# Sparse attention's half of the odd layer's output projection, unit by unit inside the attention loop

## The reference, cut to what matters

```
def odd_layer(h, ...):
    proj = rms_norm(h, norm_mix) @ w_in
    y_c = rwkv7_time_mix(proj_c, ...)              # 8 heads x 64, a state over time
    y_d = dsa_attention(q, k, v, qi, ki, wi)       # 8 query heads x 64, top-64 keys
    h = h + jnp.concatenate([y_c, y_d], axis=-1) @ w_out
    return h + moe_swiglu(rms_norm(h, norm_ffn), router, e_gate, e_up, e_down)
```

## Time and profile before

| | us |
|---|---|
| median of 3 runs | 1525.81 |
| lowest, highest | 1525.42, 1528.82 |
| span of the profiled execution | 1527.9 |
| PE busy | 1448.0 |
| DVE busy | 653.7 |
| ACT busy | 259.0 |
| POOL busy | 30.3 |

### The profile page before, as it was taken

The page is one execution under the profiler, slowest core; times in us unless marked ns, Lnnn a source line. Parts: engine busy times, 40 slices in busy tenths (PEclk is TensorE's granted clock), DMA queues, the critical chain, the costliest instruction groups (busy, mean ns, idle before and its releaser), DMA issues.

```text
span 1527.9 us, 46201 instructions
## 1 busy us (share of the span) xinstructions
PE 1448.0 (95%) x21517; PEld 1382.4 (90%) x21517; DVE 653.7 (43%) x1549; ACT 259.0 (17%) x441; POOL 30.3 (2%) x33
## 2 busy tenths in 40 slices
PE   7998999997986889999999999999999999999997
PEld 6857999997864778999999999999999999999996
DVE  6952554445467651343224224134224323332327
ACT  2333444434234210200000000000000000000001
POOL 0000000000000210000000000000000000000000
PEclk9998999999996999999999999999999999999998
DMA  9041655353330008699999999999999999999994
GB/s 312 30 166 56 220 206 181 128 198 124 126 109 1 3 3 321 236 392 406 408 395 406 409 388 408 408 381 408 408 380 410 408 376 409 406 386 408 408 373 169
DMA packets 138184, 434.27 MB, mean 284 GB/s; under 512 B 10108, under 2 KB 13286, under 8 KB 137863
## 3 DMA queue, kind: packets, MB, share of 16 engines
q1 hardware_dynamic: 133536, 420.59, 71.5%
q0 software_dynamic: 1472, 5.24, 1.0%
q10 hardware_dynamic: 2982, 5.45, 1.0%
HBM read 426.42 MB, written 4.85 MB: 282 GB/s over the span
## 4 chain that ended last, share of the span: by engine, by line
PE 85%; DMA 6%; DVE 6%; ACT 3%; issue 1%; SPq 0%; ACTq 0%; DVEq 0%
PE bank L2545 34%; PE bank L2543 18%; PE bank L2152 4%; PE bank L2154 4%; PE bank L2153 4%; DMA ring<-in_moe_w_up 4%; PE bank L1894 3%; PE bank L2222 3%; DMA ring<-in_moe_w_gate 2%; PE bank L2125 2%; PE bank L2140 1%; PE bank L2060 1%; PE bank L2145 1%; PE bank L2387 1%; DVE xnT L1083 1%
## 5 line engine op out<-in xcount | busy, mean ns | idle before, releaser
L2543 PE MATMUL bank<-ring,yT 128*32 128x384 f32 x5760 | 633.5, 490 | 7.0 <-DMA ring<-in_moe_w_gate 4.3
L2545 PE MATMUL bank<-ring,yT 128*32 128x128 f32 x5760 | 634.9, 273 | 0.0
L2545 PEld LDWEIGHTS bank<-ring,yT 128*32 128x32 f32 x5760 | 627.7, 110 | 0.4 <-issue 0.4
L2545 PE MATMUL bank<-ring,arena 128*32 128x128 f32 x2304 | 255.4, 273 | 0.0
L2543 PE MATMUL bank<-ring,arena 128*32 128x384 f32 x2304 | 255.2, 490 | 0.0
L2545 PEld LDWEIGHTS bank<-ring,arena 128*32 128x32 f32 x2304 | 251.4, 110 | 0.0
L1801 DVE TENSOR_TENSOR arena<-arena,bank 128x384 f32<-128x384 f32 x56 | 28.9, 551 | 430.6 <-PE bank L2545 286.7
L1749 DVE STREAM_TRANSPOSE arena<-arena 32x192 f32<-32x192 f32 x384 | 141.9, 370 | 114.3 <-PE bank L2545 109.3
L2543 PEld LDWEIGHTS bank<-ring,yT 128*32 128x32 f32 x5760 | 165.9, 108 | 9.7 <-issue 5.9
L2154 PE MATMUL bank<-arena_r,ring_r 128*128 128x256 f32 x608 | 171.5, 282 | 0.0
L2152 PE MATMUL bank<-arena_r,ring_r 128*128 128x256 f32 x528 | 148.0, 280 | 1.3 <-DVE arena_r L1329 1.3
(11 more groups left out here) (473 smaller groups left out, 1264.0 us busy)
## 6 DMA issues: line engine op xcount, KB each, us to landing
ring<-in_moe_w_gate SPq DMA_DIRECT2D x56, 2048.0 KB, 22.0
ring<-in_moe_w_up SPq DMA_DIRECT2D x56, 2048.0 KB, 22.1
ring<-in_moe_w_down SPq DMA_DIRECT2D x56, 2048.0 KB, 20.3
ring<-in_ffn_w_gate SPq DMA_DIRECT2D x5, 2048.0 KB, 7.9
ring<-in_ffn_w_up SPq DMA_DIRECT2D x5, 2048.0 KB, 8.1
ring<-in_ffn_w_down SPq DMA_DIRECT2D x5, 2048.0 KB, 8.6
ring<-in_o_w_in SPq DMA_DIRECT2D x5, 2048.0 KB, 7.7
ring<-in_e_w_in SPq DMA_DIRECT2D x4, 2048.0 KB, 16.9
```

The lines of the kernel that those rows point to most:

```text
L2543: pe_.matmul(b[QUAD[m], 0:FM], x(m), w[:, 0:FM], start=start, stop=stop, skip_group_check=True)
L2545: last = pe_.matmul(b[QUAD[3], P * m:P * m + P], x(m), w[:, FM:FB], start=start and m == 0, stop=stop, skip_group_check=True)
```

## The change

Inside each turn of the attention loop, between the products with the values and the transposes, PE now multiplies the unit that is finished (u-3) with its 128 rows of `w_out`, for all 8 output tiles: 8 products of 128 x 128 into banks 0 and 1 (first 128 tokens) or 2 and 3 (last). The last unit's comes after the loop, in the place of the three warming products. ACT copies the two banks into `sparse_out` (in buffers named raw and relu) once for each half of the tokens, and DVE adds them to `hT` behind L1558. The final output projection is left with the RWKV half, 4 products for each output tile. The sums of squares and half of the transposed norms move to bank 4. POOL's key mask waits for the triangles of both halves of the heads.

```diff
+    sparse_out = [L1[n][:, 0:KD * P] for n in ("raw", "relu")]
+    KK_BANKS = (4, 0)
...
             pool.wait_ge(sem("mk_raw"), t + 1)
+            pool.wait_ge(sem("T_ready"), 2 * t + 2)
             mk = sc["L"].rearrange("p (h x) -> p h x", h=HEADS)
...
+        def sparse_copy(t):
+
+            act.wait_ge(*step(f"sparse{t}_done"))
+            act.wait_ge(*((sem("acc_done"), NT) if t else (sem("shifted"), 7)))
+            for b in range(2):
+                last = act_.activation(sparse_out[t][:, 512 * b:512 * b + 512], bank[2 * t + b][:, :], ACT.Copy)
+            last.then_inc(step(f"sparse{t}_copied")[0], 1)
+
         for u in range(2, UNITS + 2):
             odd_attention(u)
+            if u == UNITS - 1:
+                sparse_copy(0)
             rwkv_step(u - RWKV_LAG)
         for u in range(UNITS + 2 - RWKV_LAG, UNITS + 2):
             rwkv_step(u)
+        sparse_copy(1)
...
-                link(v.tensor_tensor(kk2, kk2, bank[u - 6][:, :], MUL))
+                link(v.tensor_tensor(kk2, kk2, bank[KK_BANKS[u - 6]][:, :], MUL))
...
                 sem("WT_copied"), 1)
+            dve.wait_ge(*step(f"sparse{t}_copied"))
+            h_t = hT[:, :, t * P:t * P + P]
+            link(v.tensor_tensor(h_t, h_t, sparse_out[t].rearrange("p (k n) -> p k n", k=KD), ADD))
             dve.wait_ge(sem("lora_loaded"), 16 * 5)
...
                 last.then_inc(sem("pv_done"), 1)
+            if between:
+                between()
             if 1 <= u <= UNITS:
...
         def out_projection(n, behind):
             for i in range(KD):
-                if i % 4 == 0:
-                    loaded(n + i // 4)
-                for k in range(KD):
+                for k in range(KM):
...
+        def project_sparse(w):
+
+            if w < 0:
+                return
+            f, t = unit(w, UNITS)
+            if w == 0:
+                pe.wait_ge(sem("gates_done"), 1)
+                loaded(NOUT)
+                loaded(NOUT + 1)
+            pe.wait_ge(sem("o_copied"), UNITS + w + 1)
+            for i in range(KD):
+                last = pe_.matmul(bank[2 * t + i // 4][:, (i % 4) * P:(i % 4) * P + P],
+                                  view(NOUT + i // 4)[:, KM + f, (i % 4) * P:(i % 4) * P + P],
+                                  yT[:, KM + f, t * P:t * P + P], start=(f == 0 and i % 4 == 0), stop=(f == KM - 1),
+                                  skip_group_check=True)
+            if f == KM - 1:
+                last.then_inc(step(f"sparse{t}_done")[0], 1)
...
-                      lambda kt, h: Vd[:, kt, :], L1["pT"], dsa_first)
+                      lambda kt, h: Vd[:, kt, :], L1["pT"], dsa_first, between=lambda: project_sparse(u - 3))
...
                 pe.wait_ge(*step("kk_wide"))
                 for k in range(KM):
+                    if k == 2:
+                        pe.wait_ge(*step("sparse0_copied"))
                     for t in range(NT):
                         i = t * KM + k
-                        last = pe_.transpose(half(bank[k // 2], k)[:, t * P:t * P + P],
+                        last = pe_.transpose(half(bank[KK_BANKS[k // 2]], k)[:, t * P:t * P + P],
                                              sc["tmp"][:, i * P:i * P + P], ident)
                 last.then_inc(step("kk_back")[0], 1)
-        keep_warm(bank[6], WARM["tilde"])
+        project_sparse(UNITS - 1)
         pe.wait_ge(*step("tilde_done"))
+        pe.wait_ge(*step("sparse0_copied"))
...
             for hh in range(2):
+                if hh and not t:
+                    pe.wait_ge(*step("sparse1_copied"))
```

More of the change, by code:

```diff
@@ L167, in trunk @@
              "rwkv_prep": ["kk_raw", "L_done", "rk_done", "kk_inv", "tilde_done"],
-             "rwkv_act": ["kk_sq", "exps_done", "kk_norm", "kk_wide"],
+             "rwkv_act": ["kk_sq", "exps_done", "kk_norm", "kk_wide", "sparse0_copied", "sparse1_copied"],
              "routing": ["sel_ready", "m12_done", "work_ready"],
-             "rwkv_turned": ["kk_ss", "kk_back"]}
+             "rwkv_turned": ["kk_ss", "sparse0_done", "kk_back", "sparse1_done"]}
     def step(name):
@@ L910, in rwkv_step @@
                 act.wait_ge(*step("kk_ss"))
-                act_.activation(L1["st8"][:, 0:16], bank[0][:, 0:16], ACT.Sqrt).then_inc(step("kk_norm")[0], 1)
+                act_.activation(L1["st8"][:, 0:16], bank[4][:, 0:16], ACT.Sqrt).then_inc(step("kk_norm")[0], 1)
             elif u == 4:
@@ L2017, in _, with attention @@
         S5_STEPS = {"C": turn_c, "X": chunk_u, "G": turn_g, "S": chunk_states, "K": step_kernels, "out": turn_outputs}
-        def attention(u, base, q, k, vals, pT, first, p=None):
+        def attention(u, base, q, k, vals, pT, first, p=None, between=None):
             if u < UNITS:
@@ L2121, in out_projection @@
             for i in range(KD):
-                if i % 4 == 0:
-                    loaded(n + i // 4)
-                for k in range(KD):
+                for k in range(KM):
                     last = pe_.matmul(half(bank[2 + i // 2], i), view(n + i // 4)[:, k, (i % 4) * P:(i % 4) * P + P],
-                                      yT[:, k, :], start=(k == 0), stop=(k == KD - 1))
+                                      yT[:, k, :], start=(k == 0), stop=(k == KM - 1))
                 if i % 2:
@@ L2302, in _ @@
                     t, k = i // KM, i % KM
-                    last = pe_.matmul(bank[0][:, 2 * i:2 * i + 2], tmp4[:, k, t * P:t * P + P], C("pair"),
+                    last = pe_.matmul(bank[4][:, 2 * i:2 * i + 2], tmp4[:, k, t * P:t * P + P], C("pair"),
                                       start=True, stop=True)
```

## The result

| | us |
|---|---|
| before, median of 4 runs (lowest, highest) | 1527.24 (1525.42, 1528.82) |
| after, median of 4 runs (lowest, highest) | 1517.12 (1512.92, 1518.98) |
| ratio after / before, 95% interval | 0.9928 [0.9905, 0.995] |
| span of the profiled execution, before and after | 1527.9, 1514.5 |

The change is 10.1 us faster by the medians and 13.4 by the two profiled spans. The forecast was 12.4 faster, at 1513.4; the range, 1508 to 1520, holds the result. The profiled execution of the changed kernel took 1516.33, 1.8 more than its span, and in every other run where both are known the time is 1.8 to 1.9 above the span. So the profiled execution of before took about 1529.7 (an estimate from its span). That is 3.9 above the 1525.81 from which the forecast was made and outside the range of those three runs, not 2.1 above and inside it.

The account below looks back on a forecast made before the run. The prediction took PE's own order to bound the path ahead of the experts, and the weight stream, by a little, the experts. Projection -14.3, loop +4.9 and mask -3.0 gave -12.4 from 1525.8: 1513.4 us, 80% range 1508 to 1520.

Parts of the forecast that it names:

- Half of the projection: Final output projection: 64 of 128 records go at 0.2234 us each, all on the path, 14.3 us faster.
- The stream lets the gain through: Experts' weights: the stream moves with the experts' start; blocks 1 to 6 need 30.5 us and 41 are left.
- The loop: Attention loop: the sparse products added there delay RWKV's start by 4.9 us, one above the full-clock replay; bounds +2.5 and +15.2.
- full-clock replay: End of the attention loop: PE's order replayed at 2.4 GHz from turn 7, RWKV starting at 498.0 instead of 494.15, +3.85 us.
- The mask: Triangles on DVE: with POOL's mask waiting, L1539 is no longer stretched; 1.0 us gained in the first half, 2.0 in the second.
- full-clock rival: Loop and rounds: loop costs only 3.85 us, no clock fall after the triangles saves 1.5 more; 1510.8 us, chance 0.13.
- The addition, the renaming: DVE's two additions to `hT` (1.22 us each) fit into its idle time, and renaming the banks moves nothing: 0 us.
- The lower clock all the way: Attention loop: the clock stays low through all the last units, loop +15.2 us, 1523.7 in all; chance 0.05.
- the slower outcome: Loop and first half's rounds: low clock reaches into five rounds, 22.4 us lost against 17.3 saved; 1530.9, chance 0.03.
- the stream: Experts: their weight stream cannot move with its start, most of 12 us returns as PE waits; 1522 or more, chance 0.03.
- midway rival: Attention loop: the clock is up again only near 490, RWKV starts some 8 us late; 1516.5 us, chance 0.14.
- the mask's collision: POOL's mask in its new place stalls the first L1547 in each half, +4.7 us; 1518.1 us, chance 0.04.

Follow-up runs that it names:

- e8: Changed kernel with the final projection over all eight input tiles again, sparse half added twice, so another output: 1533.94 us, ratio 1.0031 to before.
- e4: Changed kernel with ACT's first copy of the sparse banks one turn earlier, in turn 6: 1515.56 us, ratio 0.9911 to before.
- e5: On top of e4, the last two units' sparse products moved behind the loop, ahead of the final projection, replacing eight warming products: 1511.93 us, ratio 0.9881 to before.
- e1: Changed kernel run again without an edit: 1519.21 us, ratio 0.9933 to before.
- e3: Changed kernel without the line that makes POOL's key mask wait for the triangles: 1521.48 us, ratio 0.9943 to before.
- e10: Changed kernel traced again without an edit, second of three such looks: 1513.79 us, beside 1528.58 for before.
- e2: Kernel before with only POOL's key mask waiting for the triangles: 1527.38 us, ratio 0.9983 to before.
- e6: Changed kernel with eight more warming products in PE's waits in turns 4 to 6 of the attention loop: 1517.33 us, ratio 0.9919 to before.
- e9: Changed kernel traced again without an edit, first of three such looks: 1517.9 us, beside 1528.58 for before.
- e11: Changed kernel traced again without an edit, third of three such looks: 1516.88 us, beside 1528.58 for before.

## Why the prediction was right, and where its sizes were off

*Half of the projection, -14.3.* Measured -13.81 between the marks. The mechanism is as forecast. A record was priced at 0.2234, from a row's 7.15, which runs to the last end; to the next row's start the same 32 records took 6.99 (590.59 to 597.58), 0.218 each, so 64 are 14.0. The slow start was 0.1 longer after. e8 isolates the term.

*The stream lets the gain through.* Right for the changed kernel. From the first expert product on it took 903.5 to 906.2 us in eleven traces of the kernels with the right output, with starts between 603 and 621 and no order by the start; before had 904.57 (and e8 908.47). PE's waits for weights come to 6.1 after and 5.6 before, all behind 1000 us.

*The loop, +4.9.* Measured +4.08 in the first trace, +4.1, +4.1, +4.8 and +5.9 in the others of this kernel: the mean is 4.6. The full-clock replay gave 3.85 and followed PE row by row: it put RWKV's start 2.7 behind `tilde_done`, the trace has 3.0, and the wait for ACT's copy, priced at 1.2 with PE as the later one, is 1.23. e4 and e5 confirm both by taking them away (1.47 and 2.03). The extra for units at the lower clock was the right kind: the clock was at 0.50 in the loop's first turns, rose behind unit 0, fell behind the sums of squares in turn 4 and rose again behind or inside unit 2. In e1, e3 and e10 it fell once more, at 480.7 to 481.5, and caught unit 3, which costs up to 1.8. The forecast had looked for the lower clock at units 3 and 4; it was at 0 and 2 in every trace, and at 3 in some.

*The mask, -3.0.* Right in size: -1.12 and -1.93 in e2, and by its ratio 2.6 with an interval of 0.8 to 4.4. In the first half I had taken 1.0 as net of ACT's second copy; net it is 0.54, since the copy costs 0.58. In the second half 2.0 was forecast for 1.93. But the second half gained 3.47 in the changed kernel, 1.54 more than the mask, and that is the clock in the rounds. Busy times and granted clock (the PEclk column) in the rounds of the second half, before, in the first trace of the changed kernel, and in e2:

```profile
540.00:543.00 3.00, 3.00 (x62) 3.00 (x62) 1.10 (x3) 0.00 (x0) 0.00 (x0) 0.50 0.00 0
536.00:545.00 9.00, 7.63 (x180) 6.59 (x180) 6.96 (x20) 3.05 (x6) 2.35 (x1) 1.00 0.01 2
538.00:540.00 2.00, 2.00 (x44) 2.00 (x42) 0.75 (x2) 0.00 (x0) 1.10 (x1) 0.50 0.00 0
```

The sum put this at nothing and left it to the full-clock rival, at 1.5. That size is right, but its reason, triangles in time, is not enough: e2 and e6 have the mask's wait too, the clock fell in their rounds, and they took 42.78 and 42.77 against 41.24. Of the ten traces with both the wait and the sparse half, e6 is the only one with that fall. What decides it stays open.

In the four cases in which the mask ran beside L1539 (before, and L1553 in e3), the stretched instruction ended 0.27 to 0.29 behind the mask, though it had started anything from 0.2 to 1.3 behind the mask's start. This agrees with the lock that the Trainium skill describes ("SBUF — State Buffer", "SBUF: two separate sides"): of a VectorE instruction with two SBUF inputs and a GpSimd one, the first holds the shared ports for its whole length and the other waits. With the wait in place the instructions with two SBUF inputs are no longer stretched, and L1562, with one, takes 0.42 to 0.45 beside a 2.35 mask. Whether the addition to `hT` would collide by the same rule was not put to the test: the two were 0.15 us apart.

*The addition, the renaming.* 0, as forecast; DVE idles 0.60 behind the addition.

*The sum.* By the marks the parts ahead of the experts sum to -13.7, against -12.4 forecast; the clock in the rounds is the term that the sum lacked. By the medians the gain is 10.1 (first runs) and 9.9 (e1), and the time is 3.7 above the forecast: 1.4 because the base of 1525.8 was too low (1527.24 with a fourth run; 33 later runs have medians of 1529.1 and 1528.8), and 2.3 because the gain was smaller. That it still lies 2.9 inside the range owes something to the range's width of 12. The two profiled spans differ by 13.4. All 38 runs of before have a median of 1528.8, and the 12 of the changed kernel 1517.8: 11.0 apart. The profiled execution of before lies 0.9 above the first, that of the changed kernel 1.5 below the second, and 0.5 of that is its loop (4.08 for a mean of 4.6). Where the rest lies in the executions that were not traced stays open.

*The rivals.* The lower clock all the way (1523.7), the slower outcome and the stream are refuted. By its number, 1517.12, the result stands nearer to the midway rival (1516.5) and to the mask's collision (1518.1) than to 1513.4, so that the forecast was the nearest is told by the traces and not by the time: RWKV's start was at most 5.9 late, not 8, with every later unit of the loop at the higher clock, and the mask did not collide. The full-clock rival's 1.5 in the rounds came in the trace, its loop of 3.85 did not quite; the -13.7 of the marks lies between it and the forecast.

## What to carry to other kernels

Work taken from an exposed stretch and put into the gaps of a latency-bound loop is gained in full only up to the last gap: here six units cost 0.6 us (e5 against before), the last two 2.0 (e4 against e5), and a wait for a copy 1.5; the last two came back by finding them a later gap. Look for the instruction that became the releaser, here PE's own order and one wait for a copy. An elementwise instruction that takes four times its usual time beside one of GpSimd is worth a look at what each reads; one wait took the stretch away. And one trace of each kernel is little: here up to 1.8 us come or go with each place at which the clock falls or not.

## What the runs showed of the hardware

The lower clock returned in the middle of the loop while PE was busy. PE in order of time in the first trace of the changed kernel, and then its busy time and granted clock (the PEclk column) in stretches of 1 us:

```profile
468.63 0.44 PE L2073 MATMUL bank<-con,ring 128*128 128x128 f32 x2 [1.63 <-DVE ring L1275]
468.91 1.85 PE L2339 MATMUL bank<-con,ring 128*128 128x2 f32 x16
470.68 0.92 PE L2047 MATMUL bank<-arena 64*128 64x256 f32 x4
471.62 0.69 PE L2057 MATMUL bank<-arena 128*64 128x128 f32 x4
472.24 3.09 PE L2309 MATMUL bank<-yT,ring 128*128 128x128 f32 x16
```

```profile
467.00:468.00 1.00, 0.00 (x1) 0.00 (x0) 0.96 (x2) 0.00 (x0) 0.00 (x0) 1.00 0.00 0
...
470.00:471.00 1.00, 1.00 (x9) 0.97 (x10) 1.00 (x4) 0.80 (x3) 0.00 (x0) 1.00 0.00 0
471.00:472.00 1.00, 0.99 (x8) 0.29 (x4) 0.74 (x2) 1.00 (x4) 0.00 (x0) 0.52 0.00 0
...
473.00:474.00 1.00, 1.00 (x7) 1.00 (x6) 0.00 (x0) 1.00 (x2) 0.00 (x0) 0.50 0.00 0
```

Ahead of the fall PE had issued 16 records of L2339, each with two moving columns, for 1.85 us, and it was busy in every stretch from 469 on; the granted clock was 1.00 and then 0.50, the level of 1.2 GHz. In every trace of this kernel unit 2's products behind it took 3.1 to 3.6 where 2.05 is usual. So PE can lose its clock while it is busy. Two things stood ahead of it in all five traces: the two-column products, and a pause of PE of 1.3 to 1.7 us (1.63 here, with the clock at 1.00) that had ended 2.4 to 3.2 us before the fall. The two-column products are not needed for it: in the same trace the clock also fell at 532.5 and 573.4, behind pauses of 1.91 and of 1.60 and 0.69, under products of 64 to 256 columns. Nor is such a pause enough: behind the one of 1.83 ahead of unit 3 the clock fell in e10, in e1 and e3 it fell inside it, and in the first trace, e9 and e11 it did not fall. What brings the fall on was not isolated.
